# Transposing 128x128 blocks on TensorE: the transpose flag in place of an fp32 product with the identity

## What is computed

```python
# per layer, pre-RMSNorm before every part
qa, ka, va, fa, qb, kb, vb = split(h @ w_in)
# A: 8 heads x 64, causal, with a forget bias; the sample tokens see 1024 cached keys too
p = softmax(where(causal, qa @ ka.T * scale + decay, NEG)); oa = p @ va
# B: 8 query heads on 2 key heads x 64, a band of 128 keys in chunks, one sink a head
p = exp(s - m) / (sum(exp(s - m)) + exp(sink - m)); ob = p @ vb
x = x + concat(oa, ob) @ w_out
# memory: 4 heads x 128 over 256 memory tokens
x = x + (softmax(qm @ mk.T * scale) @ mv) @ w_mo
# gated mixer, width 2816, with a causal convolution of width 3
x = x + (silu(conv(gate)) * val) @ w_down
```

## Time and profile before

| | |
|---|---|
| time, median of 3 runs | 3921.34 us (3921.28 to 3933.45) |
| span of the profiled execution | 3914.7 us |
| PE busy | 3472.1 us, 89% of the span |
| DVE, POOL, ACT busy | 44%, 31%, 24% |
| mean granted TensorE clock | 0.938 of full speed |

### The profile page before, as it was taken

The page is one execution under the profiler, slowest core; times in us unless marked ns, Lnnn a source line. Parts: engine busy times, 40 slices in busy tenths (PEclk is TensorE's granted clock), DMA queues, the critical chain, the costliest instruction groups (busy, mean ns, idle before and its releaser), DMA issues.

```text
span 3914.7 us, 59084 instructions
## 1 busy us (share of the span) xinstructions
PE 3472.1 (89%) x21112; PEld 3337.5 (85%) x21112; DVE 1726.9 (44%) x3290; ACT 947.4 (24%) x2236; POOL 1205.9 (31%) x984
## 2 busy tenths in 40 slices
PE   4898998777879999999969989988778799999997
PEld 3788888666869999999959879977668799999997
DVE  5442444566463333333454424454755533333335
ACT  4331332343231011011133313232432311011012
POOL 3122113116223343333431131122162243333332
PEclk9998998779989999999979999988799899999998
DMA  2111102012101111111121021111021011111111
GB/s 100 52 48 50 50 23 66 20 33 68 33 22 41 47 44 42 46 44 41 47 60 48 26 66 51 31 41 31 28 73 31 28 44 44 44 46 41 44 47 67
DMA packets 86066, 176.91 MB, mean 45 GB/s; under 512 B 10672, under 2 KB 13872, under 8 KB 85392
## 3 DMA queue, kind: packets, MB, share of 16 engines
q1 hardware_dynamic: 72416, 133.89, 12.1%
q10 hardware_dynamic: 13376, 39.15, 3.2%
HBM read 151.28 MB, written 16.29 MB: 43 GB/s over the span
## 4 chain that ended last, share of the span: by engine, by line
PE 63%; issue 20%; DVE 7%; POOL 4%; ACT 3%; DMA 2%; ACTq 0%; DVEq 0%; POOLq 0%; SPq 0%
PE PS L436 63%; POOL WH L412 3%; POOL WL L414 1%; DVE HL L1201 1%; DMA XR<-decays 1%; DVE ACC L1239 1%; ACT QH L809 1%; DVE PR L1253 1%; DMA RX<-T 0%; DVE PR L1309 0%; ACT PW L910 0%; DVE PW L1309 0%; ACT G0H L809 0%; DVE QL L1201 0%; DVE G0L L1201 0%
## 5 line engine op out<-in xcount | busy, mean ns | idle before, releaser
L412 POOL TENSOR_TENSOR WH<-RAW,zero 128x512 fp32r<-128x512 f32 x488 | 554.4, 1136 | 2636.6 <-PE PS L436 2616.9
L436 PE MATMUL PS<-HH,WH 128*128 128x384 f32 x3216 | 779.8, 338 | 121.3 <-DVE HL L1201 60.2
L436 PE MATMUL PS<-HH,WL 128*128 128x384 f32 x3216 | 770.0, 334 | 3.5 <-issue 3.5
L436 PE MATMUL PS<-HL,WH 128*128 128x384 f32 x3216 | 771.3, 335 | 0.0
L436 PEld LDWEIGHTS PS<-HH,WH 128*128 128x128 f32 x3216 | 573.9, 194 | 134.9 <-DVE HL L1201 64.2
L414 POOL TENSOR_TENSOR WL<-RAW,WH 128x512 fp32r<-128x512 f32 x488 | 655.5, 1343 | 38.3
L436 PEld LDWEIGHTS PS<-HL,WH 128*128 128x128 f32 x3216 | 578.2, 194 | 0.0
L436 PEld LDWEIGHTS PS<-HH,WL 128*128 128x128 f32 x3216 | 576.3, 193 | 0.0
L1341 DVE TENSOR_TENSOR XT<-PS,XT 128x320 f32<-128x320 f32 (+1 forms) x544 | 368.4, 719 | 380.5 <-PE PS L436 380.1
L436 PE MATMUL PS<-G0H,WH 128*128 128x384 f32 (+1 forms) x1152 | 313.0, 333 | 14.3 <-DVE G0L L1201 14.3
L436 PE MATMUL PS<-G0L,WH 128*128 128x384 f32 (+1 forms) x1152 | 311.8, 332 | 0.0
(11 more groups left out here) (176 smaller groups left out, 4815.1 us busy)
## 6 DMA issues: line engine op xcount, KB each, us to landing
RAW<-in_slabs SPq DMA_DIRECT2D x488, 256.0 KB, 2.6
XR<-decays ACTq DMA_DIRECT2D x16, 512.0 KB, 5.3
XT<-in_xT SPq DMA_DIRECT2D x8, 544.0 KB, 9.5
out_fk<-T ACTq DMA_DIRECT2D x8, 544.0 KB, 2.8
XR<-decays ACTq DMA_DIRECT2D x16, 272.0 KB, 6.8
out_fv<-T ACTq DMA_DIRECT2D x8, 544.0 KB, 2.7
RX<-T ACTq DMA_DIRECT2D x32, 136.0 KB, 2.5
out_y<-YT ACTq DMA_DIRECT2D x8, 544.0 KB, 3.1
```

Of the source, the lines that this page charges most:

```text
L412: pool.tensor_tensor(WH[:, s, :], RAW[:, s, :], zero[:, 0:1].to_broadcast([128, HALF]), ALU.add).then_inc(w_hi, 1)
L436: ins = pe.matmul(*a, **k)
```

## The change

Every block transpose is issued with TensorE's transpose flag, as `pe.transpose(out, in_, ident[:])`. Before, it was a plain float32 matmul with the block as the weights and the identity as the moving operand; the operands stay where they were, and so do the output areas, the groups, the waits and the signals. PE's program holds the same number of calls in the same order, and the other engines' programs are unchanged. The product with the causal mask (`ident_r`, in float32r) is not touched.

```diff
+            def turn_over(pe, out, in_):
+
+                ins = pe.transpose(out, in_, ident[:])
+                state["last"], state["bare"] = ins, not owed
+                if owed:
+                    ins.then_inc(owed.pop(0), 1)
...
@@ value_tiles
-                        mm(pe, PS[0:rows, b * 512 + j * 128:b * 512 + (j + 1) * 128],
-                           T32[:, tile * 128:tile * 128 + rows], ident[:], start=True, stop=True)
+                        turn_over(pe, PS[0:rows, b * 512 + j * 128:b * 512 + (j + 1) * 128],
+                                  T32[:, tile * 128:tile * 128 + rows])
...
@@ transposes
-                        mm(pe, PS[0:rows, b * 512 + j * 128:b * 512 + (j + 1) * 128],
-                           probs(st, s % 3, col, col + rows), ident[:], start=True, stop=True)
+                        turn_over(pe, PS[0:rows, b * 512 + j * 128:b * 512 + (j + 1) * 128],
+                                  probs(st, s % 3, col, col + rows))
```

## The result

The change makes the kernel **slower**, by 1.0%: 3961.1 us median of 10 runs (3930.0 to 3984.3) against 3920.1 us (3902.8 to 3933.5), a ratio of 1.0102 with a 95% interval of 1.0077 to 1.0128. The forecast was 3829 us. The profiled execution took 3971.95 us, 1.8 us above its span, and so it is in every run (1.7 to 1.9 us); the 6.6 us that I put around the span of before were mostly the distance of that execution from the median. So the two profiles lie 55.5 us apart and the medians 41 us. The ten runs of the changed kernel differ among themselves with the clock: the fastest, 3930.0 us, was granted 0.897, the slowest, 3984.3 us, 0.881.

A forecast was written before the change was run, and what follows sets the result against it. PE was taken as the bound in fox, with band heads bound by a chain through DVE and ACT. Gains of 68 + 6 + 10 + 8 = 92 us took 3921.3 to 3829 us; 8-in-10 range 3782 to 3875 us.

The forecast's parts named there:

- What bounds the kernel: PE bounds the fox attention, busy 57.50 of 58.30 us; in the band heads no engine is full.
- Two passes become one, 0.112 us each: Every block transpose, 1154 in all, drops one of two passes at an unchanged step, gaining 0.112 us.
- Cheaper pass: Rival: one pass that steps at only 0.06 us, gaining 0.164 us a block; 3787 us, chance 0.10.
- two passes still: Rival: the flag leaves two passes for a block, so nothing moves; 3921 us, chance 0.05.
- loads that no longer run ahead: Rival: a transpose's weight load waits for an empty array, up to 0.47 us a block; 4010 to 4120 us, chance 0.07.
- Fox, 68 us: 648 fox blocks save 72.6 us of passes, of which 4.5 us stay hidden at the ends of pairs.
- value hooks: Value-block transposes in 10 hooks end sooner, 0.6 us each, 6 us in all.
- The clock as a rival: PE, waiting more between shorter transposes, is granted half clock in memory, perhaps fox; 3850 to 3900 us, chance 0.08.
- PE-mode transpose: Skill page section cited for the clock: such transposes do not count as busy, so 8 us per fox window would stop counting.
- Memory, 10 us: 144 blocks in the memory heads save 16.1 us, of which 60% was taken as on the chain.
- Band, 8 us: 256 band-head blocks gain only at the end of each pair, about 1 us for each of 8 pairs.
- What it would show: Signs: 1154 records, fox window about 50 us, longer waits for `PW`; wrong if fox clock falls or `G0L` waits grow.

The follow-up runs named there:

- twice: The change, with every block transposed twice by the flag, the second over the first: 3906.1 us, 0.9966 of before.
- band: The kernel before, with the flag in the 256 band blocks alone: 3918.6 us, 1.0011 of before.
- twice_rounded: The change, with every block transposed twice by the flag and probabilities rounded to float32r, so their low part is zero: 3904.6 us, 0.9966 of before.
- weak: The change, with one plain float32r pass with its own weight load ahead of every flagged one on probabilities: 3955.0 us, 1.0089 of before.
- v32_once: The change, with fox prompt value products as one float32 product instead of three float32r ones, without DVE's split of transposed probabilities: 3853.0 us, 0.981 of before.
- r_twice: The kernel before, with probabilities rounded and each of their blocks turned by a plain float32r pass, done twice: 4241.8 us, 1.082 of before.
- mix: The change, with the next step's scores moved between the value products of two groups in fox rounds: 4027.6 us, 1.027 of before.

## Why the prediction was wrong

*What bounds the kernel:* right. PE was the bound in fox, and its slower clock went into the time.

*Two passes become one, 0.112 us each:* right. 1154 records, 7 blocks in 0.71 us, 0.10 us each. "Cheaper pass", "two passes still" and "loads that no longer run ahead" all fell.

*Fox, 68 us:* this is the step that failed, and with it the sum. The term costed the removed passes at what they took and nothing for what they did, on the ground that "in fox PE stays full". It did stay nearly full: in the second fox turn's window PE is busy 233.6 of 257.2 us after, 91%, and was 217.4 of 234.9 before, 93%. Yet its clock fell from 0.95 to 0.78. A full PE was no guard. The four windows lost 47 us where a gain of 68, and of some 5 in their value hooks, was expected: a slower clock of some 110 us and 15 us more idle time against 79 us of passes saved. The idle time is a term that the sum did not have, though the text named a part of it among its signs, PE's wait for `G0L`.

*The clock as a rival:* the right mechanism with the wrong size and place. It had 0.08 at 3850 to 3900 us, drawn from memory heads that would fall to 0.77. They fell to 0.89, and the window of heads 0 and 1 lost 3.1 us; the fox rounds, which I let in only as an "if", fell to 0.78. The text had the price, "185 us of such stretches would eat the gain"; there were 260. I let the even 1.00 of one clean fox window stand for all of fox. The whole turns had 0.91 to 0.95 in the kernel before, 136 us at half clock already, which the prediction never looked at. The rule of the Trainium skill beside this rival ("PE-mode transpose") was wrong in its reason, as `twice` shows, though what it warned of happened.

*Memory, 10 us:* wrong by its sign in the window shown, where the clock fell again (0.96 to 0.89). *Band, 8 us:* too large. The window shown gained 2.3 us, and the interval of `band` alone leaves room for a gain of 4 us at most.

*What it would show:* the sign that the forecast is wrong if the clock of the fox windows falls was the right one, and it came. PE's wait for `PW` did not grow, it is 75.6 us after 78.1. The wait for `G0L` grew from 50.5 to 70.0 us in the whole kernel, but only by 4 us in the four fox windows; the rest lies outside of them.

## What to carry to other kernels

Where TensorE is the bound, a saving of passes among narrow matmuls must be reckoned with its clock: read the granted clock of the stretch after the edit, and try the same edit with the passes put back. That shows whether the loss hangs on their number; it brings back the clock and the cover together, so the two are told apart by PE's busy and idle time in the stretch. A clean 1.00 in one window of before shows no reserve; look at the whole stretch. Where a stretch is made of narrow split products in float32r, one plain float32 product is two passes in place of three, was granted a clock at least as high here, and frees the engine that splits. This holds for 128 columns; at 256 the two float32 passes take 0.40 us, and the three float32r ones 0.36.

## What the runs showed of the hardware

The flag brings a float32 128x128 block over in one pass, at a step of 0.10 to 0.11 us, as each of the two passes of a float32 product. At full clock a narrow pass with its own weights steps so in all three forms (0.11 us for float32r); the forms differ in how they hold the granted clock, in the order of the table. I had not expected that. The contents that were tried, zeros in the low part (`twice_rounded`), made no difference. A float32 pass takes 0.20 us for 256 columns where a float32r pass takes 0.12. What the gate measures in a pass stays open: the runs rank whole kernels, and `weak` and `v32_once` say that both the form and the number of passes enter. `r_twice` differs from `twice_rounded` only in `ident_r` and in the missing flag, with rounded probabilities in both. That the order of scores and values matters too (`mix`) was seen once and is unexplained.
